# Hybrid decoder step: the steps of a prompt-attention head at other points of a mixer unit's product stream

## What is computed

```python
proj = x @ w_in_l
qb, kb, vb = moba_qkv(proj)                       # 8 heads x 128
...
s = jnp.einsum('bqhd,bqhtkd->bqhtk', qf, kg) * HEAD_DIM ** -0.5
s = s + rel_bias[t5_bucket(dist), head]
s = jnp.where(ok, s, -jnp.inf)                    # causal
p = jax.nn.softmax(s.reshape(B, Q, H, -1), axis=-1).reshape(s.shape)
return jnp.einsum('bqhtk,bqhtkd->bqhd', p, vg)
...
return jnp.concatenate([oa, ob.reshape(B, T, W_MOBA)], -1) @ w_out_l
```

## Time and profile before

| | |
|---|---|
| median of 3 runs | 1579.47 us (1577.3 to 1579.82) |
| the profiled execution | 1577.72 us, of it 1575.9 us span |
| TensorE busy | 1529.9 us, 97% of the span |
| VectorE busy | 942.8 us, 60% |
| ScalarE busy | 650.2 us, 41% |
| mean granted TensorE clock | 0.992 |

### The profile page before, as it was taken

How to read it: one execution, slowest core, us unless ns; L and a number is a source line. 1 busy time by engine, 2 the same in 40 slices (tenths; PEclk the granted TensorE clock), 3 DMA queues, 4 the chain that set the end, 5 groups by cost and what they waited for, 6 DMA issues and landing times.

```text
span 1575.9 us, 34974 instructions
## 1 busy us (share of the span) xinstructions
PE 1529.9 (97%) x14616; PEld 1485.7 (94%) x14616; DVE 942.8 (60%) x1175; ACT 650.2 (41%) x771; POOL 127.9 (8%) x145
## 2 busy tenths in 40 slices
PE   7999999999899999999999999999999999999996
PEld 7999999999799899998899999999999999999995
DVE  4445746567664356674596666666666644445566
ACT  5344343333524554464544334443333333333344
POOL 0000202121343200001000000000000000000000
PEclk9999999999999999999999999999999999999998
DMA  8788888886688965746645454556667655555453
GB/s 293 263 340 325 323 295 321 300 321 221 239 284 305 334 243 194 274 173 240 214 161 178 172 184 163 188 183 226 233 238 262 213 187 181 173 178 186 160 180 115
DMA packets 72520, 365.00 MB, mean 232 GB/s; under 512 B 9072, under 2 KB 10424, under 8 KB 45656
## 3 DMA queue, kind: packets, MB, share of 16 engines
q1 hardware_dynamic: 56960, 310.00, 54.9%
q0 software_dynamic: 13664, 52.31, 9.0%
q10 hardware_dynamic: 1792, 1.20, 0.4%
HBM read 353.20 MB, written 10.47 MB: 231 GB/s over the span
## 4 chain that ended last, share of the span: by engine, by line
PE 81%; DVE 7%; ACT 4%; SPq 3%; DMA 3%; issue 2%; DVEq 0%; ACTq 0%
PE psum_g L523 22%; PE psum_g L524 22%; PE psum_g L525 21%; PE M L2175 3%; PE M L2190 3%; DVE wl L507 2%; SPq L644 2%; ACT wh L502 2%; PE M L523 1%; PE M L525 1%; PE M L524 1%; PE psum_g L2487 1%; PE M L2301 1%; DMA pj<-x_t 1%; DMA raw<-w_out_t 1%
## 5 line engine op out<-in xcount | busy, mean ns | idle before, releaser
L523 PE MATMUL psum_g<-xh,wh 128*128 128x264 f32 (+1 forms) x2382 | 697.9, 293 | 6.7 <-DVE wl L507 3.2
L524 PE MATMUL psum_g<-xl,wh 128*128 128x264 f32 (+1 forms) x2382 | 678.0, 285 | 0.0
L525 PE MATMUL psum_g<-xh,wl 128*128 128x264 f32 (+1 forms) x2382 | 677.5, 284 | 0.0
L507 DVE TENSOR_TENSOR wl<-raw,wh 128x2048 fp32r<-128x2048 f32 (+1 forms) x205 | 461.5, 2251 | 300.0 <-ACT wh L502 298.8
L502 ACT CAST wh<-raw 128x2048 fp32r<-128x2048 f32 (+1 forms) x221 | 414.4, 1875 | 245.3 <-PE psum_g L525 197.8
L523 PEld LDWEIGHTS psum_g<-xh,wh 128*128 128x128 f32 x2382 | 450.7, 189 | 21.1 <-issue 14.7
L524 PEld LDWEIGHTS psum_g<-xl,wh 128*128 128x128 f32 x2382 | 450.9, 189 | 3.1 <-issue 2.9
L525 PEld LDWEIGHTS psum_g<-xh,wl 128*128 128x128 f32 x2382 | 449.0, 189 | 0.0
L523 PE MATMUL psum_g<-gh,wh 128*128 128x264 f32 x704 | 200.6, 285 | 0.3 <-DVE wl L507 0.3
L525 PE MATMUL psum_g<-gh,wl 128*128 128x264 f32 x704 | 199.6, 284 | 0.0
L524 PE MATMUL psum_g<-gl,wh 128*128 128x264 f32 x704 | 199.6, 283 | 0.0
(11 more groups left out here) (448 smaller groups left out, 1744.9 us busy)
## 6 DMA issues: line engine op xcount, KB each, us to landing
raw<-w_t SPq DMA_DIRECT2D x88, 1024.0 KB, 4.8
raw<-w_in_t SPq DMA_DIRECT2D x53, 1024.0 KB, 7.6
kring<-cache_k_t SPq DMA_DIRECT2D x96, 512.0 KB, 4.9
sraw<-cache_k_t SPq DMA_DIRECT2D x32, 512.0 KB, 6.5
raw<-w_out_t SPq DMA_DIRECT2D x16, 1024.0 KB, 5.2
raw<-w2a_t SPq DMA_DIRECT2D x16, 1024.0 KB, 4.8
raw<-w2b_t SPq DMA_DIRECT2D x16, 1024.0 KB, 4.9
raw<-w2c_t SPq DMA_DIRECT2D x16, 768.0 KB, 4.3
```

The costliest lines, as they stand in the source:

```text
L507: eng.tensor_tensor(wl[:, u % 2, 0:nk], raw[:, u % 2, 0:nk], wh[:, u % 2, 0:nk].bitcast(F32), ALU.subtract).then_inc(raw_used, 1)
L523: nc.tensor.matmul(out, hi_w, x_hi(k), start=(k == order[0]), stop=False)
L524: nc.tensor.matmul(out, hi_w, x_lo(k), start=False, stop=False)
L525: last = nc.tensor.matmul(out, lo_w, x_hi(k), start=False, stop=(k == order[-1]))
```

## The change

Three table entries of `beside` are moved, and the order of two names in the steps of TensorE's semaphore is swapped to match:

- `head_turn(j - 1)` goes from k = 3 to k = 4, behind one more triple.
- `head_values(j - 1)` goes from k = 6 to k = 8, behind two more triples, and so also behind `page_values` and `delta` of k = 7.
- `value_turn(j)` goes from k = 9 to k = 14, and so from in front of `head_scores(j)` (k = 13) to one triple behind it.

```diff
-        c_pe = steps("c_pe", ["tv", "sc", "tp", "oo"])
+        c_pe = steps("c_pe", ["sc", "tv", "tp", "oo"])
...
-                if k == 3 and 0 <= j - 1 < H:
+                if k == 4 and 0 <= j - 1 < H:
                     head_turn(j - 1)
-                elif k == 6 and 0 <= j - 1 < H:
+                elif k == 8 and 0 <= j - 1 < H:
                     head_values(j - 1)
...
-                    if 0 <= j < H:
-                        value_turn(j)
                     if u == KEY_UNITS + 10:
...
                 elif k == 13:
                     if 0 <= j < H:
                         head_scores(j)
+                elif k == 14:
+                    if 0 <= j < H:
+                        value_turn(j)
```

## The result

| | kernel before | changed kernel |
|---|---|---|
| median of 10 runs | 1579.32 us (1577.3 to 1583.57) | 1585.01 us (1583.2 to 1591.94) |
| ratio | | 1.0044, 95% interval 1.0029 to 1.0059 |
| profiled execution (span) | 1577.72 us (1575.9) | 1587.42 us (1585.6) |
| mean granted clock in it | 0.992 | 0.988 |

The account below looks back on a forecast made before the run. TensorE, busy for 97% of the span, was taken to bound the kernel. Terms -0.4 - 0.45 - 0.9 + 2.8 + 2.2 = +3.3 us gave 1582.8 us against a median of 1579.47; range 1578.5 to 1586.0.

Parts of the forecast that it names:

- Turn to k = 4: TensorE: a triple done in the turn's wait gains 0.4 us in unit 36 and 0.45 over units 37 to 39.
- Value turn on TensorE: Unit 36: at k = 14 the wait for VectorE's copy L1626 goes, -0.9 us.
- The table load: ScalarE, units 40 to 42: the Silu load comes onto the path, delaying the turns of units 41 to 43, +2.8 us.
- The wait for L1081 in unit 42: TensorE reaches page_values some 0.45 us early, but inside the wait for the next turn, so 0 cost.
- No drain behind a load: ScalarE: loads cost 1.28 us without 1380 ns of drain; the rival with drain had about 1587 us, chance 0.02.
- Value products to k = 8: Unit 43: the state products wait for VectorE's keep, +2.2 us, bounds 1.9 to 2.6; elsewhere 0.
- The clock: Rival: granted clock falls behind new waits in unit 42 and at state_rows(0), 1 to 1.5 us each, about 1584.2; chance 0.22.
- a half-clock stretch between 515 and 550: Sign on TensorE's granted clock: a new such stretch at 515 to 550 us would show the forecast wrong.

Follow-up runs that it names:

- f2: Changed kernel with unread matmuls filling TensorE's waits ahead of the turns of units 41, 42 and 43; 1581.38 us against 1578.52 before, ratio 1.0016.
- f0: The changed kernel measured again, as yardstick on another chip; 1585.26 us against 1578.52 before, ratio 1.0043.
- f3: Changed kernel with 8 unread matmuls only ahead of the state products; 1585.76 us against 1578.52 before, ratio 1.0040.
- e4: Changed kernel with the Silu table load of units 40 to 42 issued ahead of ScalarE's value copy; 1579.59 us against 1578.42 before, ratio 1.0006.
- e6: Changed kernel with the Silu load ahead of the value copy and unit 43's sample_delta ahead of head_out; 1574.93 us against 1578.42 before, ratio 0.9972.
- e3: Kernel before with only the turn moved to k = 4; 1577.81 us against 1578.85 before, ratio 0.9992.

## Why the prediction was right in its waits and wrong on the clock

- **Turn to k = 4.** In unit 36 right: f2 has 0.27 us of wait left there (0.3 forecast); the change's own profile has none, with half clock in front of it. In units 37 to 39 mis-sized: I took 0.15 us each and nearly the upper bound was the truth, 1.0 us for the three (0.33 each, the bound was 0.36). My argument was that the turn starts only a little later than delta's products need. In the change the triple starts 0.81 us behind those products and the turn 0.45 behind the triple, and the turn starts 1.26 us behind them instead of 1.16. Only 0.1 of the triple's 0.36 us shows up as delay of the turn. Most of the other 0.07 us is in the turn itself, which is followed by the next triple after 0.25 us (447.20 to 447.45) instead of 0.31 (445.88 to 446.19).

```profile
445.94 1.05 PE L2190 MATMUL M<-chain 128*128 128x128 f32 x8
446.75 0.37 PE L523 MATMUL psum_g<-xh,wh 128*128 128x264 f32 x1
...
447.20 0.49 PE L2281 MATMUL M<-C,kring 128*128 128x128 f32 x3
```

- **Value turn on TensorE**, -0.9: right, the wait is gone, and the step of unit 36 in f2 is -1.4 (turn and value turn, -1.3 forecast).
- **The table load**: right. ScalarE's exponentials in unit 40 start at 504.67, 4.22 us behind the copy of the values. Units 41 and 42 cost 0.9 each in f2 (0.7 and 0.9 forecast). The 0.2 us in unit 41 is a wrong link: I had L1002 start 0.3 us behind L949, and it is 0.50 (502.48 to 502.98). The wait for L1081 in unit 42 is there with 0.37 us (0.45 forecast).
- **No drain behind a load**: right. In the change too the exponential starts 0.02 us behind the end of the load (503.37 + 1.28). The Trainium skill's 1380 ns of drain ("ScalarE: Activation LUTs", "What ACT_TABLE_LOAD costs") is not in this trace.
- **Value products to k = 8**: right, 2.17 us before L2315 against 2.2. VectorE's row for `keep` and its L1626 in the change, 4.54 us apart (4.56 before):

```profile
546.09 0.42 DVE L1626 COPY qb<-M 128x256 f32<-128x256 f32 x1 [4.83 <-PE M L2288]
...
550.44 0.19 DVE L1658 COPY C<-sdec 128x64 f32<-128x64 f32 x1
```

- **The clock**: wrong, and the step that failed. The sum had 0 for it, and the forecast itself named a half-clock stretch between 515 and 550 as a sign of being wrong; the one from 526 to 532 is that. It stood as a rival with a chance of 0.22 and 1 to 1.5 us for each fall. What I leaned on, that today's waits of 0.47, 1.22 and 0.64 us leave the clock alone, said nothing about waits of 1.38, 2.17 and 1.43. The one row that did, half clock behind a wait of 2.2 us, was the nearest in size, and I should have made it the likeliest case. Measured, the clock behind the turns' waits costs 3.9 us by the medians (f0 against f2), more than the 3.1 us that the waits add; and by the mean clocks the whole change loses 5.3, of which f2 still has 1.2. A fall was also dearer than I took it, about 3.1 us in unit 42. With the 3.1 us of waits and 3.9 of clock the sum is 7.0 us; measured are 5.7 and 6.7.

The time lay in the range given, and the sign was right; 3.3 us were forecast where 5.7 and 6.7 came. That the waits alone add up so well (3.1 for 3.3) is in part luck: the turns of units 37 to 39 gave 0.5 us more than taken, and unit 41 and the state products cost about as much more.

## What to carry over

When a dense TensorE stream gets a new wait, price the wait and then price the clock behind it, from the nearest row where the engine had been idle as long; filling the wait with matmuls that nothing reads is a cheap way to learn which of the two was paid. Before moving a step that releases another engine, read that engine's order behind it up to the next thing that comes back, table loads too: a load can stand in idle time ahead of the release as well as behind it. And a few triples can be the whole of a margin: the points 5, 7 and 11 give 4.1 us where 4, 8 and 14 take 5.7.

## What the runs showed of the hardware that I had not expected

- TensorE at its lower level for about 3 and 7 us behind waits of 1.4 and 2.2 us in otherwise dense work (clock 0.50 in 508 to 511 and 526 to 529), and not in every execution: the change's runs have mean clocks from 0.988 to 0.992 in the first comparison and from 0.987 to 0.993 in f0, and f0's profile has full clock behind the wait of 1.4 us.
- A wait of the same 2.2 us at the state products gave nothing that could be measured when it was filled (f3), but some 2 us of clock when it was taken away (e4 to e6). Which of the two holds, no run here shows.
- Where TensorE is at half clock ahead of a wait whose end another engine sets, the wait is shorter. From the start of L2367 to the end of the wait for L1603 it is 13.1 to 13.2 us in every profile where I measured it. The wait is 2.9 us before and in f2, with the clock at half for some 7 us in front and full behind; 5.2 us in e3 and f3, with full clock in front and half behind; 3.9 us in the change, with some 3 us of half clock on either side. So a half-clock stretch is free in front of such a wait and paid behind it. Before:

```profile
417.00:420.00 3.00, 3.00 (x16) 0.50 0.01 4
420.00:423.00 3.00, 3.00 (x14) 0.52 0.90 280
...
427.50 1.06 PE L2301 MATMUL M<-pj 128*4 128x128 f32 x32 [2.95 <-DVE kring L1603]
```
